# Opening an encoder block with x by channels, and multiplying by the norm's roots after the products

## The chip, the core and the metric

The program runs on one core of one Trainium2 chip, in a single launch. Time is device time in microseconds. A core has five engines that run their own instruction streams and meet at semaphores: TensorE (PE; its weight loads are listed as PEld), VectorE (DVE), ScalarE (ACT), GpSimd (POOL) and SyncE (SP), which issues most DMAs here. All data is float32; the output is float32.

## The reference, cut to what matters

x has 512 tokens of 1024 channels. The block opens with

```
h    = x * rsqrt(mean(x*x over channels) + 1e-6) * norm1_g
proj = h @ w_in            # columns: 256 q_a, 128 kv_a, 32 k_rope, 512 lru_x, 512 lru_y, 2048 gates
xc   = 4-tap convolution of lru_x over tokens (per channel) + conv_b
r, i = sigmoid(xc @ w_rgate + b), sigmoid(xc @ w_igate + b)      # two directions
```

Then come two linear recurrences over tokens, latent attention with eight heads from q_a, kv_a and k_rope (both latents are normed again), gates, an output product with a residual, a second norm, a SwiGLU FFN of width 2816, and a final norm. The change is in how h and the first products of it are made; what is computed stays the same.

## The kernel before, in words

Every product runs as three matmuls in a reduced float32 format: each operand is split into a high part, written by ACT (`split_hi`, L307; `norm_hi`, L712), and a low part, the difference, written by DVE (`split_lo`, L317; `norm_lo`, L1106). PE then does low x high, high x low, high x high (`product`, L473 to L475). Weights pass through two raw slots and four split slots. A tile number counts them: T_X (0 to 3) are the lru_x columns, T_A (4 to 7) the q_a, kv_a and k_rope columns, T_G0 (8, 9) the gates of the first direction, T_Y (10 to 13) lru_y, T_V and T_G1 after. The semaphores `w_half`, `w_ready` and `w_used` count tiles split high, split low, and used; a slot is split again when its tile is used, and loaded again when its tile is split. The order on each engine is written out by hand, and an engine that waits holds back all that stands behind it.

The opening: four DMAs bring x by tokens (128 tokens a DMA, L492). ACT sums squares (L698), DVE and ACT make the roots of the norm, DVE multiplies the token rows by them (L1125), PE transposes them to channels (`transpose_half`, L1621), 16 transposes for each half of the tokens, and ACT and DVE split the transposed halves out of PSUM with the gain (hT_hi, hT_lo). PE does the four T_X tiles on 256 tokens, then on the other 256 (`half_tile`, `norm_and_tiles`). Ahead of it stand 30 transposes of the identity (L1653) that no one reads.

ACT copies the four results, one per block of 128 channels, into the padded buffer `xp` (L738). DVE convolves each block with one TENSOR_SCALAR (L1143) and three chained SCALAR_TENSOR_TENSOR (L1146), and splits T_A + n low behind block n (L317, 128x832). PE does the T_A tiles, 24 products each, then the eight products of the first gates (these need the splits of xc, L742 and L1155, and in their second half the copies `pa` of the T_A results, L1165), then T_Y with a group of 16 transposes of the normed `pa` between its second and third tile (`pa_norm`, L1203, L1204, then L1704). POOL does nothing until it multiplies the input gates by xc (`gated_input`, L617).

## Time and profile before

| | us |
|---|---|
| median of 3 runs | 678.21 (677.44 to 678.53) |
| profiled execution | 677.54 |
| its span, first to last instruction | 675.7 |
| PE busy in the span | 662.6 |
| first product of T_X starts | 11.83 |
| first product of T_A starts | 37.99 |
| first product of the gates starts | 56.11 |
| first product of T_Y starts | 62.05 |

A profile shows one execution, with busy time for each engine and what each instruction waited for. Matmuls overlap in the records: the distance from one start to the next is their cost, not the duration that stands beside them. A span starts at 0 with the first instruction, and the profiled execution is 1.8 us longer than its span.

### The profile page before, as it was taken

The numbers are of one execution on the slowest core, as the hardware profiler recorded it, in microseconds if no ns is written. First come the engines' busy times: TensorE is split into PE (matmuls) and PEld (weight loads), VectorE is DVE, ScalarE is ACT, GpSimd is POOL, SyncE is SP. The second block draws the span as 40 slices with busy tenths as digits, with TensorE's granted clock in tenths as the row PEclk, the third lists the DMA queues.
The fourth block names the chain that finished last, engine by engine and source line by source line (L and its number), as shares of the span: only waits on it lengthen the run. The fifth ranks groups of instructions, "written<-read, shape, count | busy, mean of one in ns | idle before, by whom it ended". The sixth has DMA issues, their size and how long they took to land.

```text
span 675.7 us, 10962 instructions
## 1 busy us (share of the span) xinstructions
PE 662.6 (98%) x4006; PEld 592.5 (88%) x4006; DVE 531.1 (79%) x846; ACT 403.0 (60%) x677; POOL 73.0 (11%) x72
## 2 busy tenths in 40 slices
PE   7999999999999999999999999999999999999995
PEld 6998888888888878888899999999999998888884
DVE  5686648788888886873679997888777769899896
ACT  6537678788777874232565644455554455556574
POOL 0000401110222200000000000000000003314240
PEclk9999999999999999999999999999999999999999
DMA  7333202222222326334062444422444317999903
GB/s 252 121 102 102 73 11 68 68 72 68 63 71 69 120 68 236 107 125 125 10 174 67 127 125 126 120 70 64 120 124 125 124 47 173 240 273 174 169 1 124
DMA packets 83314, 75.94 MB, mean 112 GB/s; under 512 B 6415, under 2 KB 67022, under 8 KB 83278
## 3 DMA queue, kind: packets, MB, share of 16 engines
q1 hardware_dynamic: 77246, 63.93, 31.6%
q0 software_dynamic: 6016, 11.54, 9.7%
q8 instruction: 21, 0.34, 0.2%
q14 instruction: 15, 0.12, 0.1%
q10 hardware_dynamic: 16, 0.00, 0.0%
HBM read 73.37 MB, written 2.10 MB: 112 GB/s over the span
## 4 chain that ended last, share of the span: by engine, by line
PE 90%; DVE 4%; DMA 3%; ACT 1%; issue 1%; SPq 0%; DVEq 0%
PE ps L473 15%; PE ps L475 15%; PE ps L474 15%; PE ps L1883 10%; PE ps L1886 10%; PE ps L1885 10%; PE ps L1956 4%; PE ps L1960 4%; PE ps L1958 4%; DMA scr<-in_w_ffn_down_dram 2%; PE ps L1792 2%; PE ps L1742 1%; DMA raw<-in_w_in_dram 1%; PE ps L1739 1%; DVE w_lo L1379 1%; PE ps L1621 1%
## 5 line engine op out<-in xcount | busy, mean ns | idle before, releaser
L473 PE MATMUL ps<-hT_hi,w_lo 128*128 128x512 f32 (+1 forms) x288 | 100.3, 348 | 1.9 <-DVE hT_lo L1106 1.4
L475 PE MATMUL ps<-hT_hi,w_hi 128*128 128x512 f32 (+1 forms) x288 | 98.6, 342 | 0.0
L474 PE MATMUL ps<-hT_lo,w_hi 128*128 128x512 f32 (+1 forms) x288 | 98.6, 342 | 0.0
L317 DVE TENSOR_TENSOR w_lo<-raw,w_hi 128x1024 fp32r<-128x1024 f32 (+3 forms) x55 | 64.3, 1173 | 34.0 <-ACT w_hi L307 32.7
L1883 PE MATMUL ps<-f_hi,w_lo 128*128 128x256 f32 x320 | 90.7, 283 | 0.0
L1885 PE MATMUL ps<-f_lo,w_hi 128*128 128x256 f32 x320 | 90.6, 283 | 0.0
L1886 PE MATMUL ps<-f_hi,w_hi 128*128 128x256 f32 x320 | 90.6, 283 | 0.0
L307 ACT ACTIVATE w_hi<-raw 128x1024 fp32r<-128x1024 f32 (+3 forms) x55 | 53.7, 985 | 38.7 <-PE ps L475 36.5
L942 ACT ACTIVATE w_hi<-scr 128x1024 fp32r<-128x1024 f32 x50 | 51.9, 1056 | 37.3 <-PE ps L1886 32.9
L1886 PE MATMUL ps<-hT_hi,w_hi 128*128 128x256 f32 x240 | 68.0, 283 | 0.0
L1883 PE MATMUL ps<-hT_hi,w_lo 128*128 128x256 f32 x240 | 68.0, 283 | 0.0
L1885 PE MATMUL ps<-hT_lo,w_hi 128*128 128x256 f32 x240 | 68.0, 283 | 0.0
L1415 DVE TENSOR_TENSOR w_lo<-scr,w_hi 128x1024 fp32r<-128x1024 f32 x50 | 59.5, 1221 | 6.0 <-ACT w_hi L942 5.7
L473 PEld LDWEIGHTS ps<-hT_hi,w_lo 128*128 128x128 f32 x288 | 54.5, 189 | 9.4 <-DVE w_lo L317 2.4
L1883 PEld LDWEIGHTS ps<-f_hi,w_lo 128*128 128x128 f32 x320 | 61.5, 192 | 0.1
L1886 PEld LDWEIGHTS ps<-f_hi,w_hi 128*128 128x128 f32 x320 | 61.5, 192 | 0.0
L1885 PEld LDWEIGHTS ps<-f_lo,w_hi 128*128 128x128 f32 x320 | 61.5, 192 | 0.0
L1956 PE MATMUL ps<-w_hi,f_lo 128*128 128x512 f32 x154 | 60.2, 391 | 0.3 <-DVE f_lo L1374 0.2
L475 PEld LDWEIGHTS ps<-hT_hi,w_hi 128*128 128x128 f32 x288 | 54.5, 189 | 6.3
L1960 PE MATMUL ps<-w_hi,f_hi 128*128 128x512 f32 x154 | 60.0, 389 | 0.0
L1958 PE MATMUL ps<-w_lo,f_hi 128*128 128x512 f32 x154 | 60.0, 389 | 0.0
L474 PEld LDWEIGHTS ps<-hT_lo,w_hi 128*128 128x128 f32 x288 | 54.6, 190 | 6.0
(215 smaller groups left out, 1561.0 us busy)
## 6 DMA issues: line engine op xcount, KB each, us to landing
raw<-in_w_in_dram SPq DMA_DIRECT2D x12, 1024.0 KB
raw<-in_w_ffn_gate_dram SPq DMA_DIRECT2D x12, 512.0 KB, 4.8
raw<-in_w_ffn_up_dram SPq DMA_DIRECT2D x12, 512.0 KB, 5.1
raw<-in_w_ffn_down_dram POOLq DMA_DIRECT2D x12, 512.0 KB, 9.8
...
```

What stands on the lines that cost most here:

```text
L307: last = nc.scalar.activation(split_view(w_hi, kind, t0 % 4), raw_view(kind, t0 // 2 % 2, t0 % 2), ACT.Copy)
L317: last = nc.vector.tensor_tensor(split_view(w_lo, kind, t0 % 4), raw_view(kind, t0 // 2 % 2, t0 % 2), split_view(w_hi, kind, t0 % 4).bitca ...
L473: nc.tensor.matmul(dst, l_lo, r_hi, start=start, stop=False)
L474: nc.tensor.matmul(dst, l_hi, r_lo, start=False, stop=False)
L475: return nc.tensor.matmul(dst, l_hi, r_hi, start=False, stop=stop)
L1415: nc.vector.tensor_tensor(st_split(w_lo, tile), st_source(par, tile), st_split(w_hi, tile).bitcast(F32), ALU.subtract).then_inc(w_ready, 1)
L1883: nc.tensor.matmul(dst, wl[:, k, :], x_hi[:, k, :], start=start and k == 0, stop=False, skip_group_check=True)
L1885: nc.tensor.matmul(dst, wh[:, k, :], x_lo[:, k, :], start=False, stop=False, skip_group_check=True)
L1886: last = nc.tensor.matmul(dst, wh[:, k, :], x_hi[:, k, :], start=False, stop=k == 3, skip_group_check=True)
L1956: nc.tensor.matmul(dst, f_lo[:, n % 8, tok], w_hi[:, n % 4, col], start=first, stop=False, skip_group_check=True)
L1958: nc.tensor.matmul(dst, f_hi[:, n % 8, tok], w_lo[:, n % 4, col], start=False, stop=False, skip_group_check=True)
L1960: last = nc.tensor.matmul(dst, f_hi[:, n % 8, tok], w_hi[:, n % 4, col], start=False, stop=end, skip_group_check=True)
```

## The change

- The host passes x transposed as well (`x_t`). x comes by channels, in five DMAs of 128 or 256 channels, each followed by one with the lru_x weights of the same channels. The transposes of x and the first multiplication by the roots are gone.
- ACT splits x times the gain high (`x_hi`), DVE low (`x_lo`), without roots. PE does T_X on 512 tokens: for the first four channel tiles all four result blocks side by side, for the last four one block after the other. T_A too works on x without roots.
- ACT squares x by channels. POOL adds the eight squares, seven TENSOR_TENSOR of 128x512. PE turns the sum (4 transposes), DVE reduces it, DVE and ACT make the roots, PE turns them into a row over tokens (4 transposes), and ACT copies that row to `root_row`.
- ACT copies a result block to `xp` as before, and now POOL multiplies it there by `root_row` (4 TENSOR_TENSOR of 128x512), before DVE convolves it.
- POOL then multiplies the eight channel tiles of x by the row (`x_rooted`, 8 TENSOR_TENSOR of 128x512). ACT (`h_hi`) and DVE split them for T_Y and what follows. DVE multiplies `pa` by the roots as it copies it.
- 12 transposes of the identity in place of 30. Some splits are moved: T_A + 2 and T_A + 3 high behind the splits of xc, T_G0 and T_Y later on ACT and DVE.

```diff
+    x_t_v = x_t.rearrange("(k p) n -> p k n", p=P)
...
+        x_ch = xt[:, :, :].rearrange("p t (a n) -> p (t a) n", a=2)
+        squares = scr[:, 0:KD, :]
+        root_row = store[:, 21, :]
+        def x_rooted(k):
+            return scr[:, k if k < 4 else 4 + k, :]
...
+            def load_x(n, k0, count):
+                sync.dma_start(x_ch[:, k0:k0 + count, :], x_t_v[:, k0:k0 + count, :]).then_inc(x_in[n], 16)
+            def load_wx(k0, count, done, inc=16):
+                dst = raw[:, k0 // 4, 512 * (k0 % 4):512 * (k0 % 4) + 512 * count].rearrange("p (k n) -> p k n", k=count)
+                sync.dma_start(dst, w_in_v[:, k0:k0 + count, C_LX:C_LX + W]).then_inc(done, inc)
+            load_x(0, 0, 1)
+            load_wx(0, 1, wx_in[0])
+            load_x(1, 1, 1)
+            load_wx(1, 1, wx_in[1])
+            load_x(2, 2, 2)
+            load_wx(2, 2, raw_in[0], PAIR_INC)
+            load_x(3, 4, 2)
+            load_wx(4, 2, wx_in[2])
+            load_x(4, 6, 2)
+            load_wx(6, 2, raw_in[1], PAIR_INC)
...
+            for k in range(1, KD):
+                pool.wait_ge(sq_ready, k + 1)
+                if k > 1:
+                    pool.wait_ge(sq_sum, k - 1)
+                nc.gpsimd.tensor_tensor(squares[:, 0, :], squares[:, 0, :], squares[:, k, :], ALU.add).then_inc(sq_sum, 1)
+            pool.wait_ge(row_ready, 1)
+            for n in range(NB):
+                pool.wait_ge(xp_copied, n + 1)
+                nc.gpsimd.tensor_tensor(xp[:, n, LEFT:LEFT + SEQ], xp[:, n, LEFT:LEFT + SEQ], root_row,
+                                        ALU.mult).then_inc(xp_ready, 1)
+            for k in range(KD):
+                nc.gpsimd.tensor_tensor(x_rooted(k), x_ch[:, k, :], root_row, ALU.mult).then_inc(rooted, 1)
...
+            def x_hi(k):
+                act.wait_ge(x_in[k if k < 2 else 1 + k // 2], 16)
+                nc.scalar.activation(hT_hi[:, k, :], x_ch[:, k, :], ACT.Copy,
+                                     scale=prm[:, ROW_G1 + k:ROW_G1 + k + 1]).then_inc(h_half, 1)
+            def square(k):
+                nc.scalar.activation(squares[:, k, :], x_ch[:, k, :], ACT.Square, scale=float(D) ** -0.5).then_inc(sq_ready, 1)
...
+            for k in range(2):
+                x_hi(k)
+                act.wait_ge(wx_in[k], 16)
+                nc.scalar.activation(w_hi[:, 0, 512 * k:512 * k + 512], raw[:, 0, 512 * k:512 * k + 512],
+                                     ACT.Copy).then_inc(w_half if k else wx_half, 1)
+            square(0)
+            square(1)
+            for g in range(1, 4):
+                x_hi(2 * g)
+                if g == 2:
+                    act.wait_ge(wx_in[2], 16)
+                else:
+                    act.wait_ge(raw_in[g // 2], PAIR_INC)
+                nc.scalar.activation(w_hi[:, g, :], raw[:, g // 2, 1024 * (g % 2):1024 * (g % 2) + 1024],
+                                     ACT.Copy).then_inc(w_half, 1)
+                x_hi(2 * g + 1)
+                square(2 * g)
+                square(2 * g + 1)
+            act.wait_ge(rms_ready, 2)
+            nc.scalar.activation(rstd[:, 0, 0:NT], rms[:, 0, 0:NT], ACT.Sqrt).then_inc(rstd_ready, 2)
+            def xp_copy(n):
+                if n < NB - 1:
+                    act.wait_ge(lx_done, n + 1)
+                else:
+                    tile_used(act, T_X + n)
+                nc.scalar.activation(xp[:, n, LEFT:LEFT + SEQ], ps[:, n, :], ACT.Copy).then_inc(xp_copied, 1)
+            split_hi(act, T_A)
+            act.wait_ge(s_pad, 1)
+            xp_copy(0)
+            act.wait_ge(row_turned, 1)
+            nc.scalar.activation(root_row, ps[:, 6, :], ACT.Copy).then_inc(row_ready, 1)
+            xp_copy(1)
+            split_hi(act, T_A + 1)
+            xp_copy(2)
+            xp_copy(3)
...
+            def h_hi(k):
+                act.wait_ge(rooted, k + 1)
+                tile_used(act, T_A + k // 2)
+                nc.scalar.activation(hT_hi[:, k, :], x_rooted(k), ACT.Copy,
+                                     scale=prm[:, ROW_G1 + k:ROW_G1 + k + 1]).then_inc(h_half, 1)
-                if n == 0:
+                if n < 2:
+                    split_hi(act, T_A + 2 + n)
+                if n == 2:
                     split_hi(act, T_G0)
-                if n in (2, 3):
-                    split_hi(act, T_Y + n - 2)
+                    h_hi(0)
+                    h_hi(1)
+                if n == 3:
+                    h_hi(2)
+                    h_hi(3)
+                    split_hi(act, T_Y)
+            h_hi(4)
+            h_hi(5)
+            split_hi(act, T_Y + 1)
+            h_hi(6)
+            h_hi(7)
...
+            def x_lo(k):
+                dve.wait_ge(h_half, k + 1)
+                nc.vector.scalar_tensor_tensor(hT_lo[:, k, :], x_ch[:, k, :], prm[:, ROW_G1 + k:ROW_G1 + k + 1],
+                                               hT_hi[:, k, :].bitcast(F32), ALU.mult, ALU.subtract).then_inc(h_ready, 1)
+            for k in range(2):
+                if k:
+                    dve.wait_ge(w_half, 1)
+                else:
+                    dve.wait_ge(wx_half, 1)
+                nc.vector.tensor_tensor(w_lo[:, 0, 512 * k:512 * k + 512], raw[:, 0, 512 * k:512 * k + 512],
+                                        w_hi[:, 0, 512 * k:512 * k + 512].bitcast(F32), ALU.subtract).then_inc(
+                                            w_ready if k else wx_ready, 1)
+                x_lo(k)
+            for g in range(1, 4):
+                split_lo(dve, T_X + g)
+                x_lo(2 * g)
+                x_lo(2 * g + 1)
...
+            dve.wait_ge(ss_turned, 1)
+            link(nc.vector.reduce_sum(ssq[:, 0, 0:NT], ps[:, 5, :].rearrange("p (t n) -> p t n", t=NT), AX_X))
+            link(nc.vector.tensor_scalar(mse[:, 0, 0:NT], ssq[:, 0, 0:NT], EPS, None, ALU.add))
+            nc.vector.reciprocal(rms[:, 0, 0:NT], mse[:, 0, 0:NT]).then_inc(rms_ready, 2)
+            refine(0, 0, NT, 2, done=root_ready)
+            nc.vector.sem_inc(ssq_ready, 4)
...
-                if n == 0:
+                if n == 2:
-                if n in (2, 3):
-                    split_lo(dve, T_Y + n - 2)
+                if n == 3:
+                    split_lo(dve, T_Y)
+                if t == 2:
+                    split_lo(dve, T_Y + 1)
-                nc.vector.tensor_copy(pa[:, t, 0:CA], ps[:, 4 + t, 0:CA]).then_inc(pa_ready, 1)
+                nc.vector.tensor_scalar(pa[:, t, 0:CA], ps[:, 4 + t, 0:CA], rstd[:, 0, t:t + 1], None,
+                                        ALU.mult).then_inc(pa_ready, 1)
+            for k in range(KD):
+                dve.wait_ge(h_half, KD + k + 1)
+                nc.vector.scalar_tensor_tensor(hT_lo[:, k, :], x_rooted(k), prm[:, ROW_G1 + k:ROW_G1 + k + 1],
+                                               hT_hi[:, k, :].bitcast(F32), ALU.mult, ALU.subtract).then_inc(h_ready, 1)
...
-            def cols_tile(t0, dt, bank, ks=range(KD)):
+            def cols_tile(t0, dt, bank, ks=range(KD), with_roots=False):
+                    if with_roots:
+                        pe.wait_ge(h_ready, KD + k + 1)
...
-            for n in range(30):
+            def lx_matmul(k, n, x_part, w_part, start, stop):
+                return nc.tensor.matmul(ps[:, n, :], w_part[:, k // 2, 512 * (k % 2) + P * n:512 * (k % 2) + P * n + P],
+                                        x_part[:, k, :], start=start, stop=stop, skip_group_check=True)
+            for k in range(4):
+                if k < 1:
+                    pe.wait_ge(wx_half, 1)
+                else:
+                    pe.wait_ge(w_half, k // 2 + 1)
+                pe.wait_ge(h_half, k + 1)
+                for n in range(NB):
+                    lx_matmul(k, n, hT_hi, w_hi, not k, False)
+                if k < 1:
+                    pe.wait_ge(wx_ready, 1)
+                else:
+                    pe.wait_ge(w_ready, k // 2 + 1)
+                for n in range(NB):
+                    lx_matmul(k, n, hT_hi, w_lo, False, False)
+                pe.wait_ge(h_ready, k + 1)
+                for n in range(NB):
+                    last = lx_matmul(k, n, hT_lo, w_hi, False, False)
+                if k % 2:
+                    used(last)
+            pe.wait_ge(prm_in, 16 * 8)
+            nc.tensor.transpose(ps[:, 7, 0:N_ROWS], rows[0:N_ROWS, :], ident[0:N_ROWS, 0:N_ROWS]).then_inc(prm_t, 1)
+            for n in range(NB):
+                for k in range(4, KD):
+                    if not n:
+                        pe.wait_ge(w_ready, k // 2 + 1)
+                        pe.wait_ge(h_ready, k + 1)
+                    lx_matmul(k, n, hT_hi, w_lo, False, False)
+                    lx_matmul(k, n, hT_lo, w_hi, False, False)
+                    last = lx_matmul(k, n, hT_hi, w_hi, False, k == KD - 1)
+                if n < NB - 1:
+                    last.then_inc(lx_done, 1)
+                else:
+                    used(last, 2)
+                if n == 0:
+                    pe.wait_ge(sq_sum, KD - 1)
+                    for t in range(NT):
+                        ins = nc.tensor.transpose(ps[:, 5, P * t:P * t + P], squares[:, 0, P * t:P * t + P], ident[:, :])
+                    ins.then_inc(ss_turned, 1)
+                if n == 1:
+                    pe.wait_ge(root_ready, 1)
+                    for t in range(NT):
+                        ins = nc.tensor.transpose(ps[:, 6, P * t:P * t + P],
+                                                  rstd[:, 0, t:t + 1].to_broadcast([P, P]), ident[:, :])
+                    ins.then_inc(row_turned, 1)
+            pe.wait_ge(row_ready, 1)
...
-                used(cols_tile(T_Y + m, 0, m))
+                if m == 0:
+                    used(cols_tile(T_Y + m, 0, m, with_roots=True))
+                else:
+                    used(cols_tile(T_Y + m, 0, m))
```

## Rows read from the trace of the kernel before

**Rows 1.** The page, part 1: busy us (share of the span), instructions, by engine.

```profile
PE 662.6 (98%) x4006; PEld 592.5 (88%) x4006; DVE 531.1 (79%) x846; ACT 403.0 (60%) x677; POOL 73.0 (11%) x72
```

**Rows 2.** Windows: length, then busy us per engine, PEclk, DMA share, GB/s.

```profile
11.83:37.99 26.16, 25.64 (x209) 25.25 (x210) 19.15 (x38) 14.90 (x28) 0.00 (x0) 1.00 0.33 102
37.99:56.11 18.12, 18.12 (x99) 17.95 (x97) 12.24 (x17) 5.59 (x8) 0.00 (x0) 1.00 0.48 146
56.11:62.05 5.94, 5.80 (x25) 4.43 (x24) 4.42 (x13) 5.71 (x12) 0.00 (x0) 1.00 0.35 99
62.05:88.30 26.25, 26.25 (x125) 21.97 (x124) 17.77 (x49) 18.38 (x37) 7.46 (x4) 1.00 0.21 58
```

**Rows 3.** Timeline, PE, opening: start us, us, engine line op, tiles, count.

```profile
2.79 2.82 PE L1653 MATMUL ps<-ident 128*128 128x128 f32 x12
...
6.95 0.49 PE L1653 MATMUL ps<-ident 128*128 128x128 f32 x3
```

**Rows 4.** Timeline, PE: first product, product spacings, first product of T_Y + 2.

```profile
11.83 0.36 PE L473 MATMUL ps<-hT_hi,w_lo 128*128 128x256 f32 x1 [1.25 <-DVE hT_lo L1106]
...
37.75 0.28 PE L474 MATMUL ps<-hT_lo,w_hi 128*128 128x256 f32 x1
37.87 0.28 PE L475 MATMUL ps<-hT_hi,w_hi 128*128 128x256 f32 x1
...
62.05 0.39 PE L473 MATMUL ps<-hT_hi,w_lo 128*128 128x512 f32 x1
62.28 0.39 PE L474 MATMUL ps<-hT_lo,w_hi 128*128 128x512 f32 x1
...
74.60 0.48 PE L473 MATMUL ps<-hT_hi,w_lo 128*128 128x512 f32 x1
```

**Rows 5.** Timelines of ACT and of all DMA: first x, rate by 1.75 us, copies.

```profile
4.30 1.06 ACT L698 ACTIVATE scr<-xt 128x1024 f32<-128x1024 f32 x1 [1.43 <-DMA xt<-in_x_dram]
...
29.93 0.58 ACT L738 ACTIVATE store<-ps 128x512 f32<-128x512 f32 x1
...
68.98 2.54 ACT L307 ACTIVATE w_hi<-raw 128x1024 fp32r<-128x1024 f32 x3
...
GB/s 1 289 353 374 387 402 355 254 0 45 365 86 21 287 366 0 0 0 14 0 0 0 103 196 0 0 32 294 368 349 170 0 0 0 236 199 14 0 0 0
```

**Rows 6.** Timeline, DVE: one convolution block and its split; subtractions; last pa_norm.

```profile
30.55 0.55 DVE L1143 TENSOR_SCALAR store<-store,prm 128x512 f32<-128x512 f32 x1 [0.77 <-ACT store L738]
31.13 2.33 DVE L1146 SCALAR_TENSOR_TENSOR store<-store,prm 128x512 f32<-128x512 f32 x3
33.38 1.02 DVE L317 TENSOR_TENSOR w_lo<-raw,w_hi 128x832 fp32r<-128x832 f32 x1
34.31 0.55 DVE L1143 TENSOR_SCALAR store<-store,prm 128x512 f32<-128x512 f32 x1
...
45.59 0.69 DVE L1155 TENSOR_TENSOR f_lo<-store,f_hi 128x512 fp32r<-128x512 f32 x1
46.19 1.22 DVE L317 TENSOR_TENSOR w_lo<-raw,w_hi 128x1024 fp32r<-128x1024 f32 x1
47.33 1.29 DVE L1155 TENSOR_TENSOR f_lo<-store,f_hi 128x512 fp32r<-128x512 f32 x2
...
68.04 0.28 DVE L1204 TENSOR_SCALAR store<-store,rstd 128x128 f32<-128x128 f32 x1
```

**Rows 7.** Timelines of POOL and DVE, in two stretches where both have work.

```profile
70.44 2.27 POOL L617 TENSOR_TENSOR xt<-xt,store 128x512 f32<-128x512 f32 x1
...
71.49 2.31 DVE L317 TENSOR_TENSOR w_lo<-raw,w_hi 128x1024 fp32r<-128x1024 f32 x1
...
73.72 1.77 DVE L317 TENSOR_TENSOR w_lo<-raw,w_hi 128x512 fp32r<-128x512 f32 x1
...
195.62 1.29 POOL L648 TENSOR_TENSOR xt<-xt,scr  x1 [6.14 <-DVE xt L1299]
...
196.67 0.27 DVE L1259 TENSOR_SCALAR nbias<-mx 128x2 f32<-128x2 f32 x1
```

More of the change, by code:

```diff
@@ L89, in build @@
           w_rgate, b_rgate, w_igate, b_igate, lru_lambda, w_o_lru, w_out, norm2_g, w_ffn_gate,
-          w_ffn_up, w_ffn_down, final_g, rope_q, rope_k, out):
+          w_ffn_up, w_ffn_down, final_g, rope_q, rope_k, x_t, out):
     x_v = x[0].rearrange("(t p) n -> p t n", p=P)
+    x_t_v = x_t.rearrange("(k p) n -> p k n", p=P)
     out_v = out[0].rearrange("(t p) n -> p t n", p=P)
@@ L181, in build @@
         gate_21 = scr[:, 17, 0:256]
-        x_in = [sem(f"x_in{t}") for t in range(NT)]
+        x_in = [sem(f"x_in{n}") for n in range(5)]
+        wx_in = [sem(f"wx_in{n}") for n in range(3)]
+        wx_half, wx_ready = sem("wx_half"), sem("wx_ready")
+        sq_ready, sq_sum, ss_turned, root_ready, row_turned, row_ready, rooted, lx_done, xp_copied = (
+            sem("sq_ready"), sem("sq_sum"), sem("ss_turned"), sem("root_ready"), sem("row_turned"), sem("row_ready"),
+            sem("rooted"), sem("lx_done"), sem("xp_copied"))
         x_back = sem("x_back")
@@ L274, in kind_of @@
         def kind_of(t):
-            if t < T_A or T_Y <= t < T_V:
+            if t < T_A:
+                return "plain"
+            if T_Y <= t < T_V:
                 return "cols"
@@ L725, in _ @@
-            for t in (2, 3):
-                act.wait_ge(x_in[t], 16)
-                square_sum(xt[:, t, :], 0, t, sq_junk[:, t % 2, :])
-            root(0, 2, 2, 2)
-            split_hi(act, 2)
-            split_hi(act, 3)
-            norm_hi(ROW_G1, 4, 1, 0, h_half)
+            def x_hi(k):
+                act.wait_ge(x_in[k if k < 2 else 1 + k // 2], 16)
+                nc.scalar.activation(hT_hi[:, k, :], x_ch[:, k, :], ACT.Copy,
+                                     scale=prm[:, ROW_G1 + k:ROW_G1 + k + 1]).then_inc(h_half, 1)
@@ L733, in _ @@
+            act.wait_ge(row_turned, 1)
[4 more added lines that the diff above has]
+            xp_copy(3)
             act.wait_ge(lam_neg, 1)
             nc.scalar.activation(sp[:, 1, :], sp[:, 0, :], ACT.Exp).then_inc(lam_exp, 1)
-            act.wait_ge(s_pad, 1)
-            for n in range(NB):
-                tile_used(act, T_X + n)
-                nc.scalar.activation(xp[:, n, LEFT:LEFT + SEQ], ps[:, n, :], ACT.Copy).then_inc(xp_ready, 1)
-                split_hi(act, T_A + n)
+            def h_hi(k):
[3 more added lines that the diff above has]
+                                     scale=prm[:, ROW_G1 + k:ROW_G1 + k + 1]).then_inc(h_half, 1)
@@ L895, in _ @@
             split_hi(act, T_FFN + 1)
[L896 removed]
+            norm_hi(ROW_G2, 0, 0, 0, h2_half)
             split_hi(act, T_FFN + 2)
@@ L903, in _ @@
             split_hi(act, T_FFN + 3)
-            norm_hi(ROW_G2, 0, 1, KD, h2_half)
+            norm_hi(ROW_G2, 0, 1, 0, h2_half)
             def act_hi(n):
@@ L1635, in half_tile @@
                 return last
-            def norm_and_tiles(src, count, base, t0, bank, h_sem):
-                for j in range(4):
-                    half_tile(t0 + j, bank + j, 0, h_sem if not j else None)
-                    if j == 1:
-                        transpose_half(src, count, 1, base)
-                for j in range(4):
-                    used(half_tile(t0 + j, bank + j, 1, h_sem if not j else None))
-                    if j == 0:
-                        pe.wait_ge(prm_in, 16 * 8)
-                        nc.tensor.transpose(ps[:, 7, 0:N_ROWS], rows[0:N_ROWS, :],
-                                            ident[0:N_ROWS, 0:N_ROWS]).then_inc(prm_t, 1)
@@ L1652, in _ @@
-            for n in range(30):
-                nc.tensor.transpose(ps[:, 6, 0:P], ident[:, :], ident[:, :])
-            pe.wait_ge(prm_ready, 1)
-            transpose_half(xt, 0, 0, 4)
-            norm_and_tiles(xt, 0, 4, T_X, 0, h_ready)
+            for n in range(12):
+                nc.tensor.transpose(ps[:, 6, 0:P], ident[:, :], ident[:, :])
+            def lx_matmul(k, n, x_part, w_part, start, stop):
+                return nc.tensor.matmul(ps[:, n, :], w_part[:, k // 2, 512 * (k % 2) + P * n:512 * (k % 2) + P * n + P],
+                                        x_part[:, k, :], start=start, stop=stop, skip_group_check=True)
@@ L1995 @@
     tab_q, tab_k = rope_constants()
-    for name, a in [(n, inputs[n]) for n in _INS] + [("rope_q", tab_q), ("rope_k", tab_k)]:
+    for name, a in [(n, inputs[n]) for n in _INS] + [("rope_q", tab_q), ("rope_k", tab_k),
+                                                         ("x_t", np.asarray(inputs["x"])[0].T)]:
         a = np.ascontiguousarray(a)
```

45 lines of the change are left out of this document (3 added, 42 removed).

## The prediction

> **What bounds the kernel now.** The page's busy shares come first: PE works in 98% of the span [rows 1]. What is worth something is then only what PE does, and where it waits. The windows by stage say where: of the 26.16 us from the first T_X product to the first of T_A, PE is busy 25.64, the T_A stage of 18.12 has no gap, the gates lose a little, and 62.05 to 88.30 is full [rows 2]. The one large hole is ahead: the first product starts at 11.83 [rows 4]. So the change can win there, some 6 us, and what it takes away from PE in the T_X stage. But a kernel in which PE always has work depends on its suppliers being ahead of it. In the T_A stage DVE is busy 12.24 of 18.12 and POOL 0.00 [rows 2]. I look next at what a busy POOL does to DVE, since the change gives POOL 19 instructions in a stretch where it had none.
>
> The rows where both have work answer that [rows 7]. A POOL multiplication of 128x512 alone takes 1.29 us; next to DVE's splits it takes 2.27, and DVE's splits 2.31 in place of 1.22. The starts tell how: POOL at 70.44, DVE at 71.49, the next DVE at 73.72. They take turns, and each waits until the other's instruction is over. DVE loses 2.31 - 1.22 = 1.09 us per turn for a large instruction, and 1.09 for a small one too (1.77 for 128x512; a like one alone is 0.69 [rows 6]). What is lost is POOL's instruction, whole. Where POOL has a backlog, every DVE instruction with two SBUF inputs costs 1.0 to 1.1 us more. I take 1.02 (1.09 less the gap between DVE's own instructions, in which POOL has already begun).
>
> **The change, part by part.** All times are from the start of the span.
>
> *Start of the products.* The DMAs deliver 289 GB/s in the first filled slice and 353 to 402 after [rows 5]. The first 256 KB of x are in at about 3.5 (512 KB were by 4.30 [rows 5]), and each further 256 KB takes 0.68 us. ACT splits x at 3.5 to 4.1 and w at 4.2 to 4.8. The twelve identity transposes start at 2.79 and the last starts before 5.2 [rows 3], so PE begins at 5.35. That is 6.5 us earlier than 11.83. If x comes as late as 4.3 it is 0.8 us less. The ten load issues take SP some 4.5 us instead of 2.8, ahead of data that take 11 us to move; the small parameter rows are then due at 17 and not at 29, behind 4 MB that are in by 14 [rows 5]. I cost both at nothing.
>
> *T_X, PE's part.* 96 products of 512 columns at 62.28 - 62.05 = 0.2275 (mean over the stretch) make 21.84 us, against 192 of 256 columns at 0.12 [rows 4], 23.04. Nine transposes at some 0.11 [rows 3] and their turnaround cost 1.1; before there were 16 in this stage. Until about 6.6 PE is at the low clock: the twelve transposes start every 0.213 us, the later three every 0.11 [rows 3]. That costs 0.6.
>
> *T_X, its suppliers.* DVE has 2 splits of 128x512, 3 of 128x1024 and 8 of x: 2 x 0.61 + 3 x 1.14 + 8 x 0.65 = 9.8 us by the start distances of [rows 6]. POOL's seven additions fall among them, as ACT delivers squares. Laid end to end from 4.8, with 6 turns lost at 1.02 and 2.0 us of waiting for ACT and the loads, DVE ends at 22.7. PE would need the last of it at about 19: it waits 0.6, 1.0 and 2.1, 3.7 us together. T_X then takes 21.84 + 1.1 + 0.6 + 3.7 = 27.2 and ends at 32.6, against 37.99. The lead is down to 5.4. At no lost turn these waits are nearly nothing and it ends at 28.9.
>
> *The root row.* Block 0 is done at 23.5, since PE has waited. Turning the sum (0.45), the reduction (0.7, by the 0.69 of a 128x512 [rows 6]), two small instructions, ACT's root and the refinement end at 26.1, before PE is through block 1 at 26.7. Turning the row costs PE 0.45, and ACT copies it by 27.7 (0.58 [rows 5]). PE has work all that time: no wait.
>
> *The convolution.* This is the step that decides. Before, a block took DVE 34.31 - 30.55 = 3.76 us, its split included [rows 6], beside a PE tile of 18.12 / 4 = 4.53 [rows 2]; and DVE started at 30.55 with PE due at 37.99, a lead of 3.6 us once the first tile was split. Now POOL starts at 27.7. Its four block products and eight `x_rooted` products follow each other without a wait that lasts. Each of DVE's five instructions of a block has two SBUF inputs, or is a TENSOR_SCALAR between SBUF tensors. For the last kind I go by the small one at 196.67, which ends at 196.94, with POOL's at 195.62 + 1.29 = 196.91 [rows 7]: it waits too. Block 0: 1.3 for POOL, 3.85 for DVE, four turns lost: the first T_A tile is split at 37.0. PE is ready at 32.6 and waits 4.5. Block 1 loses five turns: 3.85 + 5.1 = 8.95, split at 46.0. PE, done with its tile at 41.6, waits 4.4. In block 2 POOL's last two instructions go by (its twelfth ends at 48.7): 3.85 + 2.0, at 51.9, PE waits 1.4. Block 3 is ready at 55.7, before PE. T_A ends at 32.6 + 18.1 + 10.2 = 60.9, against 56.11: a lead of 5.4 has become a loss of 4.8.
>
> The Trainium skill (SBUF — State Buffer, "Who interferes with whom") says that such a `tensor_scalar` in a two-port mode holds the same pair of ports as GpSimd, and that one with two SBUF inputs contends with a GpSimd instruction that reads SBUF. By that rule the four TENSOR_SCALAR wait like the rest; if they did not, T_A would end 1.8 us earlier.
>
> *Gates, T_Y.* The gates take 24 x 0.2275 = 5.5 in place of 5.94: the wait before their second half goes, since T_Y + 1 is no longer split ahead of all `pa` copies. T_Y's first tile needs the eight new `h_lo`: 8 x 0.65 = 5.2 us on DVE, each done just before PE is at it. But the norm of `pa` stands behind them. Before, it ended at 68.32 [rows 6], 4.6 us ahead of its transposes (74.60 less 1.66 for them [rows 4]). It comes 5.3 later against the end of T_A and PE 0.4 earlier: a wait of 1.1. ACT's splits of T_Y + 2, at 68.98 [rows 5], slide along, and DVE's low one meets POOL's `gated_input`: another 0.8. Sum 1.9, less 0.4: the loss of 4.8 is 6.3 at the end of T_V. Behind that PE waits as little as before, and order and lengths are unchanged; nothing gives it back.
>
> **Sum.** Start -6.5, T_X +1.1 (27.2 less 26.16), T_A waits +10.2, gates -0.4, T_Y +1.9: +6.3. The profiled execution of 677.54 (its span of 675.7 and 1.8 around it) becomes 683.8; by the median of the runs, 0.7 higher, 684.5.
>
> **Rivals.** *The turns are not lost, or POOL yields (faster).* Then T_X ends at 28.9, the first T_A tile is split at 29.2, and DVE's 3.76 per block stays inside PE's 4.53. T_A ends at 47.3 and T_V at 79.5, against 88.30: 8.8 us less, 669.4. Some 17 turns are counted above, 6 in T_X and 11 in the convolution; laid out again with 0.65 a turn, both kernels end T_V together, so it decides below that. Against it are all the rows of both engines together [rows 7].
>
> *Half the turns.* If DVE gets two instructions in for each one of POOL's, the same twelve spread over more blocks, and each block hides 0.7 in PE's slack. The T_X waits fall by 1.8, T_A ends near 55.6, and the whole is about +1: 679.2. For it: chained instructions have gaps in which the order could slip. Against it: at 70.44 to 75 the turns are strict.
>
> *PE's clock falls in the new holes.* At 2.79 to about 6.6 PE ran at the low level, 1.2 GHz, after it had done nothing [rows 3]; the granted clock is 1.00 in every later stage [rows 2], and no gap there is longer than the 1.3 us before 11.83. Two holes of over 4 us are new. Some 4 us at half speed lose 2.0. After the first hole the wait for the second tile hides that, after the second all but 0.6 of it. With a slow T_X opening too, some +8: 686. The Trainium skill (TensorE: Matmul & The Clock Gate, "The HAM clock gate") says that an idle array falls back to the lower clock; no row here shows it. It would take the sum to 685 to 686.
>
> **From this to the numbers.** The sum as it stands 0.60; with a clock that falls 0.13; half the turns 0.14; no turns lost 0.13. This kernel's runs can tell 0.2%, 1.4 us, from nothing. Slower: 0.60 + 0.13 and more than half of the third, 0.81. Same 0.05, faster 0.14. The likeliest case's own range is 680.5 (a turn of 0.9 us, or no wait of TENSOR_SCALAR, and a little more) to 687 (x late, clock). Down to 676 takes in the third case, up to 689 a longer hole in T_X.
>
> **What would show it.** The first product near 5.4 and T_X over by 31 to 34. Every L1146-like instruction of blocks 0 and 1 at 1.7 to 1.9 us in place of 0.75, none in block 3; POOL's twelve products at some 1.8 from start to start. PE waiting for the splits of T_A and T_A + 1, 4 us each, and for `pa_norm`. From 95 on the same distances as before, 6 us later. I am wrong if the convolution takes 0.78 per step beside POOL (then it is the first rival), or if PE is held up in T_X by over 6 us, for the loads or the row.

## The result, and the profile after

The changed kernel takes 688.68 us (median of 4 runs, 687.96 to 689.0), the kernel before 677.99 (now of 4 runs, 677.44 to 678.53): a ratio of 1.0156, 95% interval 1.0139 to 1.0174. It is slower by 10.7 us where 6.3 was forecast. The profiled execution took 687.96, its span is 685.8.

The page of the kernel after, busy us by engine, beside [rows 1]:

```profile
PE 663.8 (97%) x3868; PEld 587.2 (86%) x3868; DVE 548.4 (80%) x835; ACT 408.0 (59%) x678; POOL 104.3 (15%) x91
```

DVE has 11 instructions fewer than before and is busy 17.3 us longer. That is the first sign: the engine that supplies PE does less and takes longer for it.

The windows of the same stages answer to [rows 2]: T_X with PE's wait behind it, the first tile of T_A, the second, the last two, and on from the gates. Columns: length, then busy us of PE, PEld, DVE, ACT and POOL, granted clock, DMA share, GB/s.

```profile
4.90:39.27 34.37, 26.79 (x108) 20.77 (x106) 25.02 (x28) 19.14 (x31) 18.57 (x12) 0.93 0.45 157
39.27:47.68 8.41, 7.38 (x24) 6.76 (x25) 8.30 (x6) 1.79 (x3) 8.41 (x6) 0.66 0.00 0
47.68:54.24 6.56, 4.81 (x25) 4.42 (x25) 6.45 (x6) 0.96 (x2) 4.23 (x3) 1.00 0.28 80
54.24:64.96 10.72, 10.72 (x48) 10.54 (x49) 7.68 (x11) 5.33 (x9) 0.00 (x0) 0.84 0.58 178
64.96:98.40 33.44, 32.20 (x149) 26.43 (x149) 28.12 (x70) 25.74 (x51) 7.45 (x4) 1.00 0.25 70
```

T_A, 39.27 to 64.96, now takes 25.69 us where it took 18.12 without a gap. In the window where POOL is busy throughout (39.27 to 47.68), DVE is nearly so too, with 8.30 of 8.41 us. And the granted clock is below 1.00 in three of the five; before it was 1.00 in all of [rows 2].

PE's timeline, at the milestones of [rows 4] and at each wait. Columns: start, us, engine, line, operation, tiles, count, and in brackets the idle time and what ended it.

```profile
4.90 1.63 PE L1737 MATMUL ps<-hT_hi,w_hi 128*128 128x512 f32 x3
...
18.24 0.47 PE L1737 MATMUL ps<-hT_hi,w_lo 128*128 128x512 f32 x1 [0.78 <-DVE hT_lo L1195]
...
23.81 0.47 PE L1737 MATMUL ps<-hT_hi,w_lo 128*128 128x512 f32 x1 [2.95 <-DVE hT_lo L1195]
...
39.27 0.68 PE L490 MATMUL ps<-w_hi,hT_lo 128*128 128x416 f32 x1 [3.09 <-DVE w_lo L334]
...
47.68 0.45 PE L490 MATMUL ps<-w_hi,hT_lo 128*128 128x416 f32 x1 [1.03 <-DVE w_lo L334]
...
54.24 0.46 PE L490 MATMUL ps<-w_hi,hT_lo 128*128 128x416 f32 x1 [1.75 <-DVE w_lo L334]
...
64.96 0.40 PE L490 MATMUL ps<-f_hi,w_lo 128*128 128x512 f32 x1
...
82.02 1.97 PE L1836 MATMUL ps<-ident,store 128*128 128x128 f32 x16 [0.53 <-DVE store L1295]
...
84.70 0.47 PE L490 MATMUL ps<-hT_hi,w_lo 128*128 128x512 f32 x1 [0.71 <-DVE w_lo L334]
```

Every wait that decides ends with an instruction of DVE. The first product is 6.93 us earlier than before (11.83). T_X with the wait behind it takes 34.37 in place of 26.16, +8.2; T_A +7.6; from the gates to the first product of T_Y + 2 it is 19.74 in place of 18.49, +1.25. Together 84.70 - 74.60 = +10.10, and PE's last product starts at 678.74 against 668.65, +10.09. All of the loss is made ahead of 85 us, and nothing after gives any back.

What DVE did in the convolution, timeline, to be read against the 3.76 us block of [rows 6]:

```profile
32.53 1.49 DVE L1228 TENSOR_SCALAR store<-store,prm 128x512 f32<-128x512 f32 x1 [3.26 <-POOL store L656]
34.06 3.23 DVE L1231 SCALAR_TENSOR_TENSOR store<-store,prm 128x512 f32<-128x512 f32 x3
37.20 1.92 DVE L334 TENSOR_TENSOR w_lo<-raw,w_hi 128x832 fp32r<-128x832 f32 x1
39.04 1.50 DVE L1228 TENSOR_SCALAR store<-store,prm 128x512 f32<-128x512 f32 x1
40.58 5.01 DVE L1231 SCALAR_TENSOR_TENSOR store<-store,prm 128x512 f32<-128x512 f32 x3
45.51 2.11 DVE L334 TENSOR_TENSOR w_lo<-raw,w_hi 128x832 fp32r<-128x832 f32 x1
47.55 1.51 DVE L1228 TENSOR_SCALAR store<-store,prm 128x512 f32<-128x512 f32 x1
49.09 4.16 DVE L1231 SCALAR_TENSOR_TENSOR store<-store,prm 128x512 f32<-128x512 f32 x3
53.17 1.02 DVE L334 TENSOR_TENSOR w_lo<-raw,w_hi 128x832 fp32r<-128x832 f32 x1
54.10 0.54 DVE L1228 TENSOR_SCALAR store<-store,prm 128x512 f32<-128x512 f32 x1
```

The starts of the blocks are 6.51, 8.51 and 6.55 us apart, and the last block is at its old pace. In units of 0.95 us (1.50 less 0.55) the three lost 3, 5 and 3 turns (a turn is the time that one DVE instruction loses to one POOL instruction). The unit is less than the 1.29 us that such a POOL instruction takes alone [rows 7]. POOL's side of it:

```profile
8.53 1.40 POOL L652 TENSOR_TENSOR scr<-scr 128x512 f32<-128x512 f32 x1 [6.96 <-ACT scr L758]
11.73 11.38 POOL L652 TENSOR_TENSOR scr<-scr 128x512 f32<-128x512 f32 x6 [1.80 <-ACT scr L758]
31.40 2.34 POOL L656 TENSOR_TENSOR store<-store 128x512 f32<-128x512 f32 x2 [8.28 <-ACT store L794]
...
38.20 13.71 POOL L659 TENSOR_TENSOR scr<-xt,store 128x512 f32<-128x512 f32 x8
```

POOL ends at 51.91. DVE's first instruction at the old length starts after that, at 53.17. In T_X the last six additions take 1.90 each where the first, nearly alone, takes 1.40, and DVE is slowed beside them.

The clock, three windows of the kernel after (columns as above; 0.50 is the level of 1.2 GHz):

```profile
24.54:27.96 3.42, 3.42 (x11) 2.82 (x11) 0.98 (x3) 0.00 (x0) 0.00 (x0) 0.50 0.73 273
38.20:45.02 6.82, 5.75 (x17) 5.52 (x18) 6.71 (x5) 1.44 (x3) 6.82 (x6) 0.50 0.00 0
55.26:58.68 3.42, 3.42 (x12) 3.30 (x11) 3.35 (x6) 2.47 (x5) 0.00 (x0) 0.50 0.01 2
```

Ahead of the first PE had waited 0.78, 0.76 (at 19.93, not shown) and 2.95 us. The second began inside the wait of 3.09, 2.0 us after PE's last product had ended at 36.18. Ahead of the third were waits of 1.03 and 1.75 us, and it began when PE had been at work again for 1.0 us. The Trainium skill (TensorE: Matmul & The Clock Gate, "The HAM clock gate") has it that an idle array falls back to the lower clock: this trace agrees, the one of before could not show it.

### The profile page after: what moved, and what is told of

It is laid out like the page before. It is cut to its first block, busy times and chain, and to the rows that moved or that the text cites. A ratio compares the mean times of both kernels' runs of the same rounds, so it can differ in the third digit from the quotient of the medians.

```text
span 685.8 us, 10719 instructions
## 1 busy us (share of the span) xinstructions
PE 663.8 (97%) x3868; PEld 587.2 (86%) x3868; DVE 548.4 (80%) x835; ACT 408.0 (59%) x678; POOL 104.3 (15%) x91
## 4 chain that ended last, share of the span: by engine, by line
PE 76%; DVE 10%; issue 6%; DMA 4%; ACT 2%; POOL 1%; SPq 0%; DVEq 0%; POOLq 0%; ACTq 0%
PE ps L490 12%; PE ps L491 12%; PE ps L492 12%; PE ps L2015 8%; PE ps L2018 8%; PE ps L2017 8%; PE ps L2088 4%; PE ps L2092 4%; PE ps L2090 4%; DVE w_lo L334 2%; DVE store L1231 2%; DMA scr<-in_w_ffn_down_dram 2%; PE ps L1924 2%; DMA raw<-in_w_in_dram 2%; PE ps L1874 1%
## 5 line engine op out<-in xcount | busy, mean ns | idle before, releaser
L334 DVE TENSOR_TENSOR w_lo<-raw,w_hi 128x1024 fp32r<-128x1024 f32 (+3 forms) x54 | 67.3, 1249 | 29.0 <-ACT w_hi L324 26.0
L490 PE MATMUL ps<-hT_hi,w_lo 128*128 128x512 f32 (+1 forms) x224 | 81.6, 364 | 0.9 <-DVE w_lo L334 0.7
L492 PE MATMUL ps<-hT_hi,w_hi 128*128 128x512 f32 (+1 forms) x224 | 80.5, 359 | 0.0
L491 PE MATMUL ps<-hT_lo,w_hi 128*128 128x512 f32 (+1 forms) x224 | 80.4, 359 | 0.0
L700 POOL DMA_DIRECT2D raw<-in_w_ffn_down_dram x12 | 14.6, 1216 | 344.6 <-DVE w_lo L1470 344.6
L324 ACT ACTIVATE w_hi<-raw 128x1024 fp32r<-128x1024 f32 (+3 forms) x51 | 49.5, 978 | 28.5 <-PE ps L492 23.9
L490 PEld LDWEIGHTS ps<-hT_hi,w_lo 128*128 128x128 f32 x224 | 42.3, 189 | 8.1 <-issue 1.5
L492 PEld LDWEIGHTS ps<-hT_hi,w_hi 128*128 128x128 f32 x224 | 42.3, 189 | 6.3
```

The source lines that it names most:

```text
L334: last = nc.vector.tensor_tensor(split_view(w_lo, kind, t0 % 4), raw_view(kind, t0 // 2 % 2, t0 % 2), split_view(w_hi, kind, t0 % 4).bitca ...
L490: nc.tensor.matmul(dst, l_lo, r_hi, start=start, stop=False)
L491: nc.tensor.matmul(dst, l_hi, r_lo, start=False, stop=False)
L492: return nc.tensor.matmul(dst, l_hi, r_hi, start=False, stop=stop)
```

## The experiments

The leading theory, call it turns: next to a POOL instruction that reads SBUF, each DVE instruction with two SBUF inputs (or a TENSOR_SCALAR) waits while one POOL instruction runs, and PE waits for DVE. Its rivals: the chain of new dependences through ACT and POOL is late by itself; DVE simply has more work; the fall of the clock is the main cost. Medians of the changed kernel and of all twelve experiments, each beside the kernel before as it was measured together with it:

| kernel | us | over before, us | ratio (95%) |
|---|---|---|---|
| after | 688.68 | +10.7 | 1.0156 (1.0139 to 1.0174) |
| e1_roots_late | 684.73 | +6.2 | 1.0096 (1.0079 to 1.0113) |
| e2_no_roots | 682.89 | +4.4 | 1.0059 (1.0038 to 1.0079) |
| e3_adds_on_dve | 684.14 | +5.7 | 1.0085 (1.0068 to 1.0102) |
| e4_clock_fill | 686.80 | +8.3 | 1.0130 (1.0107 to 1.0153) |
| e5_mult_from_psum | 685.76 | +7.6 | 1.0119 (1.0099 to 1.0138) |
| e6_one_add | 682.46 | +4.3 | 1.0065 (1.0048 to 1.0081) |
| e7_three_moves | 678.91 | +0.7 | 1.0008 (0.9999 to 1.0017) |
| e8_no_gpsimd | 675.00 | -3.2 | 0.9955 (0.9941 to 0.9968) |
| e9_before_plus_pool | 688.26 | +10.1 | 1.0142 (1.0115 to 1.0170) |
| e10_before_plus_memset | 681.06 | +2.9 | 1.0051 (1.0036 to 1.0067) |
| e11_three_and_softplus | 678.67 | +0.4 | 1.0009 (1.0000 to 1.0018) |
| e12_softplus_later | 686.02 | +7.8 | 1.0115 (1.0100 to 1.0131) |

**The kernel before, with GpSimd made busy (e9).** Nobody reads what POOL computes here, so no dependence is added.

```diff
+ nc.gpsimd.memset(scr[:, 0:2, :], 1.0).then_inc(s_fill, 1)
...
+ pool.wait_ge(xp_ready, 1)
+ for n in range(12):
+     if n > 1: pool.wait_ge(s_fill, n)
+     nc.gpsimd.tensor_tensor(scr[:, 2 + n % 2, :], scr[:, 0, :], scr[:, 1, :], ALU.mult).then_inc(s_fill, 1)
...
```

> The kernel before, unchanged but for twelve products of 128x512 on GpSimd that no one reads, started when the first recurrent input is copied. Turns theory: the convolution of blocks 0 and 1 goes from 3.76 to 8 to 9 us, TensorE waits in T_A, and it is 6 to 9 us slower than before, 684 to 687, though GpSimd's work is on no chain. Rival (chain of dependences): 678, no change.

DVE and then POOL of e9, timelines:

```profile
30.37 0.55 DVE L1153 TENSOR_SCALAR store<-store,prm 128x512 f32<-128x512 f32 x1 [0.76 <-ACT store L748]
30.95 5.07 DVE L1156 SCALAR_TENSOR_TENSOR store<-store,prm 128x512 f32<-128x512 f32 x3
35.95 2.12 DVE L318 TENSOR_TENSOR w_lo<-raw,w_hi 128x832 fp32r<-128x832 f32 x1
37.99 1.51 DVE L1153 TENSOR_SCALAR store<-store,prm 128x512 f32<-128x512 f32 x1
```

```profile
30.49 20.34 POOL L632 TENSOR_TENSOR scr<-scr 128x512 f32<-128x512 f32 x12 [28.04 <-ACT store L748]
```

DVE's first instruction had started 0.12 us before POOL and kept its 0.55; each one after it costs 0.9 to 1.1 more. Twelve products on no chain at all cost 10.1 us, more than the 6 to 9 expected: the gates start at 62.34 in place of 56.11, T_Y + 2 at 85.14 in place of 74.60. The rival "chain of dependences" cannot make this. That the sum equals the change's own is partly chance: here 4.3 us come behind 62, by waits of 2.1 for `f_lo` and 0.7 for `pa` at 66.63 and 68.27, where the changed kernel loses 1.25 between the same marks.

**The eight root products after the convolution (e1).**

```diff
+ pool.wait_ge(xc_full, NB)
  for k in range(KD):
      nc.gpsimd.tensor_tensor(x_rooted(k), x_ch[:, k, :], root_row, ALU.mult).then_inc(rooted, 1)
```

> The changed kernel, but GpSimd starts its eight x_rooted products only when the last convolution block is done. Turns theory (GpSimd and VectorE exclude each other, one instruction each in turn): blocks 1 and 2 of the convolution fall from about 8.4 and 7.5 us to 4.5 and 3.8, the T_A stage ends 6 to 7 us earlier, at about 58.3 in place of 65.0; T_Y then waits some 3 us for the late x_rooted. Net 3 to 5 us faster than the changed kernel, 684 to 686. Rival (the loss comes from the longer chain of dependences, not from two engines at once): the same work in the same order on each engine, later on GpSimd: no gain in T_A, T_Y later, slower than 688.7. Clock theory: also gains, since two holes close.

DVE of e1, timeline, the second block and what meets the eight products later; then POOL:

```profile
38.72 0.53 DVE L1229 TENSOR_SCALAR store<-store,prm 128x512 f32<-128x512 f32 x1
39.29 2.33 DVE L1232 SCALAR_TENSOR_TENSOR store<-store,prm 128x512 f32<-128x512 f32 x3
...
49.98 5.18 DVE L1241 TENSOR_TENSOR f_lo<-store,f_hi 128x512 fp32r<-128x512 f32 x3
55.09 2.31 DVE L334 TENSOR_TENSOR w_lo<-raw,w_hi 128x1024 fp32r<-128x1024 f32 x1
```

```profile
49.21 15.52 POOL L660 TENSOR_TENSOR scr<-xt,store 128x512 f32<-128x512 f32 x8 [11.29 <-DVE store L1232]
```

With POOL silent, blocks 1 to 3 are 3.76 apart again and T_A has no wait inside: the gates start at 57.50, 7.5 us earlier than in the kernel after. 3.1 of it goes again by T_Y + 2 (80.38, 4.3 earlier), since the products now meet the `f_lo` subtractions and the splits, and PE waits for `pa`, DVE L1252, 2.1 us and for the sigmoids, ACT L836, 1.7. The turns move with the POOL work.

**The eight products left out (e2).**

```diff
- for k in range(KD):
-     nc.gpsimd.tensor_tensor(x_rooted(k), x_ch[:, k, :], root_row, ALU.mult).then_inc(rooted, 1)
...
```

The splits for T_Y still run, on the squares that lie in the same buffer, and they wait for the root row in place of the products. So T_Y and what follows work on other values, and T_Y's dependence on POOL is gone too.

> Leaves out the eight x_rooted products: what is split again for T_Y and after are the squares of x, not x times the roots; the two splits still run. Turns theory: T_A as in e1_roots_late, and T_Y has nothing to wait for: 6 to 8 us faster than the changed kernel, 681 to 683, still slower than before. Rival (chain of dependences): 1 us at most, 688.

Blocks 1 to 3 are again 3.76 apart, T_A begins at 39.92, the gates at 59.65, T_Y + 2 at 78.94, 5.8 earlier than after. Its six runs spread over 4 us. In its profile the clock was low from 20.8 to 27.6 and from 41.3 to 44.7, and DVE waited 3.1 us ahead of its third split of weights (1.8 in the kernel after), so its T_X ends later than in the kernel after, and all of its 6.3 us come behind that, in the stretch where the eight products stood.

**Where the squares are added (e3, e6).** e3 gives the seven additions to DVE. e6 leaves six of them out and does only the last, on POOL, so its roots are not those of the norm.

```diff
- (POOL) nc.gpsimd.tensor_tensor(squares[:, 0, :], squares[:, 0, :], squares[:, k, :], ALU.add)
+ (DVE)  nc.vector.tensor_tensor(squares[:, 0, :], squares[:, 0, :], squares[:, k, :], ALU.add)
...
```

> The seven additions of squares on VectorE in place of GpSimd: 4.6 us more work for VectorE in the T_X stage. Turns theory: six lost turns (6.1 us) go and 4.6 us come, spread where VectorE had slack; T_X ends about 3 us earlier, at 32 to 33 in place of 36, and its holes shrink, so the clock holds too: 3 to 5 us faster than the changed kernel, 684 to 686. Rival (VectorE simply has too much work): slower by up to 4.6 us, 689 to 693.

> Leaves out six of the seven additions of squares (the roots are wrong). Turns theory: VectorE loses no turn in T_X, T_X ends at about 30 in place of 36 and the clock holds there: 5 to 7 us faster than the changed kernel, 682 to 684. Rival (chain of dependences or loads): under 1 us.

e3 gives DVE more to do and is 5 us faster than the kernel after (ratios 1.0085 and 1.0156): T_A begins at 35.08 in place of 39.27. That ends the rival by which DVE is just overloaded. The low part of `x` was the wait of 4.5 us in T_X; it is 0.3 in e3 (with a new one of 1.2 for the sum, DVE L1206) and 1.4 in e6. In T_A e3 waits as long as the theory wants, up to 3.1 us, because the twelve products are still beside the convolution (blocks 6.52, 8.50 and 6.55 apart). e6 begins T_A at 33.55, 5.7 earlier, and ends 6.4 better.

**How much is the clock (e4).** PE turns identities in the holes, 88 in all.

```diff
+ def keep_busy(count, bank):
+     for _ in range(count): nc.tensor.transpose(ps[:, bank, 0:P], ident[:, :], ident[:, :])
+ ...  (block 0, k 6: 24; ahead of T_A: 24; of T_A + 1: 32; of T_A + 2: 8)
```

> The changed kernel with 88 more transposes of the identity on TensorE, placed in its holes (24 before the sixth channel tile, 24, 32 and 8 before the first three T_A tiles), so that it is hardly idle. Turns theory with the clock as a second, smaller cost: the granted clock stays at 1.00 from about 7.5 on, the holes stay, and 1.5 to 3 us come back: 686 to 687. If the clock were the main cost, nearly all 10 us would come back, 679.

Three windows of e4 (its T_X, T_A, gates to T_Y + 2):

```profile
4.90:37.93 33.03, 30.57 (x156) 25.23 (x154) 25.02 (x28) 19.04 (x31) 17.32 (x12) 1.00 0.46 162
37.93:62.15 24.22, 23.12 (x137) 22.39 (x138) 22.02 (x20) 6.65 (x11) 12.77 (x8) 1.00 0.26 78
62.15:83.41 21.26, 19.05 (x90) 14.93 (x88) 18.38 (x57) 18.60 (x38) 2.51 (x2) 1.00 0.25 74
```

The granted clock is 1.00 in all three windows, and the kernel is 1.8 us faster by the ratios (1.0156 less 1.0130) and by the spans of the profiled pair (685.8 and 684.0). The intervals of the two ratios overlap (1.0139 to 1.0174, 1.0107 to 1.0153), so this is the size of the effect to within some 2 us and no more. It is what the low clock costs net, less the fillers' own cost, which no run separates. What it rules out is the rival by which the clock is the main cost: 8.3 of the 10.7 us stay with the clock full. The three stretches of low clock hold more than 1.8 in slower products. In the profiles e4 is 2.8 us ahead at the gates (62.15 and 64.96) but 1.3 at T_Y + 2 (83.41 and 84.70), where it meets waits of 0.58, 0.92 and 0.71: part of what a fast clock gives back is waited away again.

**Does POOL collide by reading or by writing (e5, e10).** e5 has DVE multiply the recurrent input straight out of PSUM, so the four ACT copies and four POOL products go. e10 is the kernel before with POOL work that only writes.

```diff
- (ACT)  nc.scalar.activation(xp[:, n, LEFT:LEFT + SEQ], ps[:, n, :], ACT.Copy)
- (POOL) nc.gpsimd.tensor_tensor(xp[:, n, LEFT:LEFT + SEQ], xp[:, n, LEFT:LEFT + SEQ], root_row, ALU.mult)
+ (DVE)  nc.vector.tensor_tensor(xp[:, n, LEFT:LEFT + SEQ], ps[:, n, :], root_row, ALU.mult)
...
```

```diff
+ pool.wait_ge(xp_ready, 1)
+ for n in range(12):
+     if n > 1: pool.wait_ge(s_fill, n - 1)
+     nc.gpsimd.memset(scr[:, 2 * (n % 2):2 * (n % 2) + 2, :], 1.0).then_inc(s_fill, 1)
```

> The four root products before the convolution by VectorE, straight out of PSUM (one SBUF input), in place of ScalarE's copy and GpSimd's product; x_rooted stays on GpSimd behind the row. Turns theory: GpSimd still has eight instructions beside the convolution, so eight turns are lost and VectorE has 2.9 us more: T_A ends 2 to 5 us earlier than in the changed kernel, 684 to 688. The product out of PSUM is not held up and takes about 0.7 us beside GpSimd. Rival (any VectorE instruction waits for GpSimd): it takes 1.8.

> As e9_before_plus_pool, but with twelve memsets of 128x1024 on GpSimd, which read nothing. If what is shared is the reading side alone, only the TENSOR_SCALAR in its fast mode could wait: under 1 us, 678 to 679. If any two instructions of the engines exclude each other, a loss of several us like e9, by the length of the memsets.

DVE of e5, while POOL multiplies without a pause (30.85 to 43.73):

```profile
30.87 0.69 DVE L1223 TENSOR_TENSOR store<-ps,store 128x512 f32<-128x512 f32 x1 [2.73 <-ACT store L788]
31.60 0.83 DVE L1226 TENSOR_SCALAR store<-store,prm 128x512 f32<-128x512 f32 x1
32.47 5.03 DVE L1229 SCALAR_TENSOR_TENSOR store<-store,prm 128x512 f32<-128x512 f32 x3
```

DVE, then POOL of e10:

```profile
30.61 1.25 DVE L1151 TENSOR_SCALAR store<-store,prm 128x512 f32<-128x512 f32 x1 [0.76 <-ACT store L746]
31.90 2.32 DVE L1154 SCALAR_TENSOR_TENSOR store<-store,prm 128x512 f32<-128x512 f32 x3
...
35.08 6.87 DVE L1151 TENSOR_SCALAR store<-store,prm 128x512 f32<-128x512 f32 x1
```

```profile
30.63 11.03 POOL L630 MEMSET scr<- 128x1024 f32 x12 [29.07 <-ACT store L746]
```

The product out of PSUM takes 0.69 beside a busy POOL: one SBUF input, no wait. Three accumulations with two SBUF inputs take 5.03. Beside POOL's writes the same three take 2.32, their old time. The TENSOR_SCALAR behind the product lost only 0.28 (0.83 in place of 0.55), and 0.23 in the next block, so not every meeting costs a full turn. The gates of e5 start at 60.35, 4.6 earlier than in the kernel after, T_Y + 2 at 81.64, 3.1 earlier. So for the instructions with two SBUF inputs it is POOL's reading that collides. The Trainium skill (SBUF — State Buffer, "Who interferes with whom") says just that: a DVE instruction with two SBUF inputs contends with a GpSimd instruction that reads SBUF and not with one that only writes, and one with a single SBUF input outside the two-port modes doesn't; both runs agree. The size of the other part of e10 was not expected, and is why it lost 2.9 us and not under one: a TENSOR_SCALAR is held up by a POOL that only writes as well. The one at 35.08 took 6.87 us, until POOL's last memset was over at 41.66. PE waited 2.5 for the split behind it.

**All three cures together (e7), and POOL idle (e8).** e7 is e1, e3 and e5 in one. e8 is e7 with the eight root products left out, and the squares split in their place, as in e2.

> e1_roots_late, e3_adds_on_dve and e5_mult_from_psum together: GpSimd is idle until the last convolution block is done. Turns theory: T_X ends near 32, no wait in T_A, TensorE never idle long enough there for its clock to fall; the late x_rooted costs some 5 us of waits between T_A and T_Y. About 9 us faster than the changed kernel: 679 to 681, that is, the kernel before again. If the three gains overlapped for another reason than the turns, the sum would be far smaller: 683 to 685.

> As e7_three_moves, but the eight x_rooted products are left out (the squares are split in their place), so GpSimd has nothing to do until the input gates. Turns theory: the whole gain of the opening shows, some 13 us faster than the changed kernel and 2 to 4 us faster than before, 674 to 676. If the order of dependences in the new opening were the cost, it would be no faster than before: 678 or more.

e7 comes out level with the kernel before: 1.0008, interval 0.9999 to 1.0017, 11 runs against 21. Of the 10.7 us, 10 are gone. e7's T_A runs from 33.03 to 51.2 without a gap; what is left stands in its next DVE rows:

```profile
46.24 5.19 DVE L1245 TENSOR_TENSOR f_lo<-store,f_hi 128x512 fp32r<-128x512 f32 x3
51.36 2.28 DVE L334 TENSOR_TENSOR w_lo<-raw,w_hi 128x1024 fp32r<-128x1024 f32 x1
```

In e8 the same three subtractions take 1.89 and the split 1.22. PE of e7 waits 2.42 us, to 53.74, and the split ends at 53.64. e8 is 3.9 us faster than e7 and 3.2 faster than before: with POOL idle in this stretch the early opening is worth 3.2 us, and the eight products, at the later of the two places tried, cost more than that (3.9).

**The decay constants out of the way (e11, e12).** Eighteen small DVE instructions ahead of the norm of `pa` are moved behind the splits of T_Y + 2, in e7 (e11) and in the changed kernel (e12).

```diff
- link(nc.vector.tensor_scalar(r, e, 2.0, None, ALU.add)) ... decay[:, k, :]   (ahead of mean(1, 0, NT, QL, 3 * NT))
+ the same lines, behind the loop of split_lo(dve, t)
```

> e7_three_moves, with VectorE's chain of seventeen small instructions for the decays (3.4 us) behind the norm of pa and its three weight splits. If the last step of the prediction is right (h_lo pushes pa_norm past TensorE), 1.5 to 2 us faster than e7_three_moves: 677 to 679, equal to the kernel before or a little faster.

> The changed kernel with the same move of the decay chain alone. The waits for pa_norm and for the T_Y + 2 weights (0.9 and 1.0 us) go: 1.5 to 2 us faster than the changed kernel, 686.7 to 687.2. If those waits came from elsewhere (ScalarE's sigmoids, the clock): no change, 688.7.

e11 is e7 within the noise, where 1.5 to 2 us of gain were expected: from the gates to T_Y + 2 22.68 us and 22.86. e12 did take away both waits, for `pa_norm` and for T_Y + 2, and won 0.56 of their 1.24 in that stretch (19.18 and 19.74); a wait of 0.6 for `pa` appears at 69.88. By the medians the move is worth 2.9 us (7.8 and 10.7 over before, ratios 1.0100 to 1.0131 and 1.0139 to 1.0174); the profiled pair shows 0.6 of it (last product at 678.13 and 678.74). The difference lies in which executions were profiled: that of e12 is its slowest of four (687.33, median 686.02), that of the changed kernel its fastest (687.96, median 688.68), and the two medians of the kernel before differ by 0.25. What the faster executions of e12 did better than the profiled one no trace shows; their mean granted clock was 0.987 to 0.992, its own 0.985.

## Why the prediction was right in kind and short in size

The median of 688.68 lies above the range of the likeliest case (680.5 to 687) and just inside the outer bound of 689, which the prediction gave for a longer hole in T_X. The direction and the mechanism were right; 4.4 us of the 10.7 were not in the sum (3.8 by the profiled pair).

*Start of the products.* Predicted 5.35, came at 4.90: 0.45 better. But the first eight products were slow, 3.12 us from 4.90 to 8.02 where eight at 0.2275 take 1.82. That is 1.3 lost in place of the 0.6 in the sum, so the earlier start gave nothing.

*T_X, its suppliers.* The step was right in kind: six turns on DVE (three pairs of `x` splits at 2.4, 3.5 and 2.4 in place of some 1.4, two splits of w at 2.3 in place of 1.2), and PE waits of 0.8, 0.8 and 3.0 where 0.6, 1.0 and 2.1 were forecast. Mis-sized was the term "2.0 us of waiting for ACT and the loads": DVE waits 1.27 us for the second split of w and 1.77 for the third, 3.0 together, a turn costs 1.06 here, and DVE is through at 24.3 and not 22.7. Left out was the low clock: from 24.54 to 27.96 PE ran at half speed. The root row then took 5.4 us from the end of block 0 (25.89 to 31.3) where 4.2 was worked out, 0.6 of it the turning of the sum at the low clock (1.06 for four transposes, 0.45 forecast), and the row's own turning stood 0.8 behind three products. POOL began at 31.40, 3.7 us late. That moved the first split of T_A from 37.0 to 39.1, though one turn less fell on it. The stage, 34.37 for 31.65, is +2.7 of the 3.8 us that were missing in the trace.

*The convolution.* Right in sum: 4 + 5 + 2 turns forecast, 3 + 5 + 3 measured, eleven in both. Their price was 0.95, against 1.02 taken; "POOL's instruction, whole" is too much, since it takes 1.29 alone. The TENSOR_SCALAR lost its turn as well (1.50 in place of 0.55). Forecast were PE waits of 4.5, 4.4 and 1.4; measured 3.09, 1.03 and 1.75. The first is shorter because PE came to it 3.6 us late (36.2 and not 32.6) and DVE only 2.1. The second is shorter because PE was slower in between, at the low clock: from 39.27 the tile took 7.38 us for what took 4.53. That the loss from the end of T_X to the gates, 3.09 + 7.57 = 10.7 us, comes near the 10.2 of the forecast is luck in its parts: 5.9 of it are waits, the rest mostly slow products. T_A from its first product to the gates is 25.69, where 23.9 (60.9 less 37.0) was written.

*The clock.* This was given 0.13 as a rival, and it happened, at each of the two long holes and once after two short ones. The rival said some +8 in place of +6.3, 1.7 more; e4 puts its net price at 1.8 us, to within some 2. It should have stood in the main case: a forecast with two holes of 4 us in a stage that had none already contained the idle PE. By stages the missing 3.8 is 2.7 (T_X) + 1.8 (T_A) - 0.45 (start) - 0.25 (gates and T_Y, below). By causes, e4 gives the clock some 1.8 of it, over both stages. The other 2.0 is put down to the slow first products, the late supply of T_X and the later row; no run separates these.

*Gates and T_Y.* +1.5 forecast, +1.25 measured, with 0.53 for `pa_norm` (1.1) and 0.71 for T_Y + 2 (0.8). e12 shows that taking both away wins 0.56 there.

*The signs named.* The first product came near 5.4 and the twelve POOL products at 1.7 from start to start, as written. T_X was to be over by 31 to 34 and was over at 36.2; the waits for T_A and T_A + 1 were to be 4 us each and were 3.1 and 1.0; in block 0 one of the three accumulations was slowed and not all; and the kernel stands 10 us later from 95 on, not 6.

*The rivals.* That no turns are lost is refuted in every run in which POOL reads beside DVE; e8, in which none can be lost, gives 675.0 and not the 669.4 of that rival. The additions then take DVE 7 x 0.65 = 4.6 us and its four PSUM products 2.8; how much of the gap these explain was not measured. Half the turns is refuted by the count. Dependences alone and an overloaded DVE are refuted by e9 and e3. What is shown: POOL's instructions that read SBUF are the cause: 10.0 of the 10.7 us are gone when they stand elsewhere or on DVE (e7), and 13.9 when there are none (e8). Argued only, not separated by a run: how the 1.8 us of clock divide between the stages, and what each of the other late terms cost.
